# Index planes turned a tile at a time, and constant products ahead of TensorE's waits

## The reference, cut to what matters

```python
sc = einsum('thid,ikd->thik', q, keys)               # 8 heads, 2 halves, 128 keys each
top_s, top_i = top_k(sc, 16)
cand_s = top_s[:, :, 0, :, None] + top_s[:, :, 1, None, :]
best_s, best_pos = top_k(cand_s.reshape(c, 8, -1), 16)
idx = ...                                            # expert i * 128 + j
gate = softmax(best_s)
act = gelu(einsum('td,thkd->thk', xc, u[idx]))
out = einsum('thk,thkd->td', gate * act, v[idx])
```

## Time and profile before

| | |
|---|---|
| three runs | 2798.41, 2799.45, 2804.3 us |
| profiled execution's own time | 2799.7 us |
| its span | 2798.0 us |
| busy: PE, DVE, ACT, POOL | 2708.4, 1826.1, 927.0, 340.7 us |
| mean granted clock of PE | 0.989 |
| PE busy, 500 to 1160 us | 630.0 of 660 |
| PE busy, 1320 to 1430 us (groups of layer 0) | 104.7 of 110 |
| PE busy, 1430 to 1850 us (main loop of layer 0) | 416.5 of 420, DMA share 0.93 |
| TensorE's wait for ScalarE (L2637) before 1315.89 us, early blocks | 2.00 us |
| POOL's last gather issue before the one-hots | 1313.41 us |

### The profile page before, as it was taken

One profiled execution on the slowest core, in us unless ns is written; L12 is line 12 of the kernel. 1 busy time (PEld: TensorE's weight loads), 2 busy tenths in 40 slices (PEclk: granted clock), 3 DMA queues, 4 the chain that ended last, 5 costly groups with the idle time before them and its releaser, 6 DMA issues.

```text
span 2798.0 us, 46131 instructions
## 1 busy us (share of the span) xinstructions
PE 2708.4 (97%) x17120; PEld 2473.6 (88%) x17120; DVE 1826.1 (65%) x3984; ACT 927.0 (33%) x1975; POOL 340.7 (12%) x409
## 2 busy tenths in 40 slices
PE   8999999999999899998999999999999989999998
PEld 4888888778888788898999999977889989999998
DVE  6888888746665687679854454447867887445442
ACT  4222222324674566412521110126752144111001
POOL 0000000000000000001831121100000156111210
PEclk9999999999999999999999999999999999999999
DMA  7333233222323233369469999942344865999995
GB/s 300 112 122 127 106 122 142 71 95 96 136 73 109 91 117 139 125 232 381 177 247 383 378 395 420 402 145 106 113 153 174 347 231 196 358 379 376 419 421 195
DMA packets 86356, 609.20 MB, mean 218 GB/s; under 512 B 9584, under 2 KB 9968, under 8 KB 13744
## 3 DMA queue, kind: packets, MB, share of 16 engines
q1 hardware_dynamic: 60480, 420.23, 39.9%
q0 software_dynamic: 25712, 186.79, 16.9%
HBM read 605.93 MB, written 1.05 MB: 217 GB/s over the span
## 4 chain that ended last, share of the span: by engine, by line
PE 83%; DVE 9%; issue 3%; ACT 2%; DVEq 2%; DMA 1%; ACTq 0%; POOL 0%; POOLq 0%
PE bank L2538 21%; PE bank L504 10%; PE bank L506 10%; PE bank L505 10%; PE bank L2528 7%; PE bank L2477 4%; PE bank L2500 4%; PE bank L2513 3%; PE bank L1690 3%; DVE arena L2582 1%; PE bank L1007 1%; PE bank L996 1%; PE bank L1380 1%; PE bank L1398 1%; DVE res L2587 1%
## 5 line engine op out<-in xcount | busy, mean ns | idle before, releaser
L2538 PE MATMUL bank<-arena,wring 128*128 128x176 f32 x4096 | 626.4, 313 | 4.0 <-DVE arena L2860 4.0
L2538 PEld LDWEIGHTS bank<-arena,wring 128*128 128x128 f32 x4096 | 614.4, 190 | 6.8 <-issue 6.3
L488 DVE TENSOR_TENSOR peer_r<-wring,peer_r 128x512 fp32r<-128x512 f32 x440 | 296.2, 697 | 213.2 <-ACT peer_r L483 210.0
L504 PE MATMUL bank<-h_r,peer_r 128*128 128x512 f32 (+1 forms) x1088 | 395.9, 364 | 4.9 <-DVE h_r L518 3.3
L2595 POOL DMA_INDIRECT arena<-in_experts,arena x160 | 174.7, 1092 | 1718.8 <-DVE arena L2813 1001.7
L506 PE MATMUL bank<-h_r,peer_r 128*128 128x512 f32 (+1 forms) x1088 | 383.6, 353 | 0.0
L483 ACT ACTIVATE peer_r<-wring 128x512 fp32r<-128x512 f32 x440 | 266.6, 628 | 231.1 <-PE bank L506 225.9
L505 PE MATMUL bank<-h_r,peer_r 128*128 128x512 f32 (+1 forms) x960 | 333.0, 347 | 0.0
L2582 DVE SCALAR_TENSOR_TENSOR arena<-arena,res 128x1024 f32<-128x1024 f32 x128 | 156.8, 1225 | 267.9 <-DMA arena<-in_experts,arena 266.6
L2477 PE MATMUL bank<-res,wring 128*128 128x176 f32 x1920 | 288.1, 313 | 4.0 <-ACT arena L2637 4.0
L2477 PEld LDWEIGHTS bank<-res,wring 128*128 128x128 f32 x1920 | 286.6, 190 | 5.3 <-issue 4.8
(11 more groups left out here) (423 smaller groups left out, 4031.4 us busy)
## 6 DMA issues: line engine op xcount, KB each, us to landing
wring<-in_w_peer SPq DMA_DIRECT2D x256, 1024.0 KB, 8.1
wring<-in_w_proj SPq DMA_DIRECT2D x34, 1024.0 KB, 4.8
wring<-in_w_hy SPq DMA_DIRECT2D x32, 1024.0 KB, 5.0
arena<-in_w_ada POOLq DMA_DIRECT2D x16, 1024.0 KB, 5.0
wring<-in_w_out SPq DMA_DIRECT2D x16, 1024.0 KB, 4.8
wring<-in_w_ada SPq DMA_DIRECT2D x8, 1024.0 KB, 9.8
wring<-in_w_hyout SPq DMA_DIRECT2D x8, 1024.0 KB, 4.8
wring<-in_w_q SPq DMA_DIRECT2D x8, 1024.0 KB, 4.8
```

Source lines behind the costliest of these rows:

```text
L488: v.tensor_tensor(SPLIT[:, buf, 1, :], raw_quarter(name, i, j, q), SPLIT[:, buf, 0, :].bitcast(F32), ALU.subtract).then_inc(split_lo, 1)
L504: pe.matmul(out_ap, w_hi, x_hi, start=start, stop=False, **kw)
L2538: mm = pe.matmul(expert_sum(k), w[:, k * P:(k + 1) * P], gates, start=False, stop=True, skip_group_check=True)
```

## The change

New places of constant products: 5 ahead of the last `back` of the convolution, 3 between heads and `at_out`, 4 ahead of norm0, and in each layer 2 between `values_tensor` and split chunk 4, 3 ahead of the norm behind the mixer, 3 between the fold and the norm behind the experts.

In the expert layer the planes of tile 0 are turned and copied on their own, right behind the planes products in the middle of the early blocks. `pair_ready` counts tiles. VectorE makes the one-hots of groups 0 and 1 behind part 14 of `route(1)`, so ahead of the last L2790. GpSimd makes its own when tile 0 is there. ScalarE makes them behind the last early block, then copies tile 1. TensorE turns tile 1 ahead of group 2. VectorE and GpSimd wait for tile 1 from group 12 on. The tables TV, TIU, TIF of the routing move 4096 words further, out of the way of the one-hots.

```diff
-        c6 = Carve(BLOCKS * T)
+        c6 = Carve(BLOCKS * T + 2 * UNITS * UNIT)
...
-            hyena_tiles(pe, head, tail, back, first=first)
+            hyena_tiles(pe, head, tail, back, first=first, ahead_of_last=lambda: keep_clock(pe, 5, 5))
...
         def norm0_tensor(pe):
+            keep_clock(pe, bank_of("at_out", 0, KT - 1)[0], 4)
             tokens_tensor(pe, 0, "at_out")
...
                 mm.then_inc(fold_done, 1)
+            keep_clock(pe, 4, 3)
             tokens_tensor(pe, 2 * l + 2, f"post{l}")
...
             values_tensor(pe, l)
+            keep_clock(pe, bank_of(f"proj{l}", 0, 4)[0], 2)
             proj_split(pe, l, 4)
...
+            def pair_turn(tt):
+                pe.wait_ge(ijg_ready, 2 * l + tt + 1)
+                for q in range(3):
+                    mm = pe.transpose(bank[2 + tt][:, q * P:(q + 1) * P], IJG[:, q, tt * P:(tt + 1) * P], ident)
+                mm.then_inc(ijt_done, 1)
...
                 if n == PLANES_AFTER:
                     planes()
-
-            pe.wait_ge(ijg_ready, 2 * (l + 1))
-            for tt in range(2):
-                for q in range(3):
-                    mm = pe.transpose(bank[2 + tt][:, q * P:(q + 1) * P], IJG[:, q, tt * P:(tt + 1) * P], ident)
-                mm.then_inc(ijt_done, 1)
+                    pair_turn(0)
...
             for n in range(GROUPS):
                 b, x = n % 4, GROUPS * l + n
+                if n == 2:
+                    pair_turn(1)
                 pe.wait_ge(hot, HOT0 + x + 1)
...
+            def pair_in(tt):
+                act.wait_ge(ijt_done, 2 * l + tt + 1)
+                act.activation(PAIR[:, :, tt * P:(tt + 1) * P], view(bank[2 + tt][:, 0:3 * P], 3),
+                               ACT.Copy).then_inc(pair_ready, 1)
...
+                    pair_in(0)
...
-            for tt in range(2):
-                act.wait_ge(ijt_done, 2 * l + tt + 1)
-                a = act.activation(PAIR[:, :, tt * P:(tt + 1) * P], view(bank[2 + tt][:, 0:3 * P], 3), ACT.Copy)
-            a.then_inc(pair_ready, 1)
-            act.drain()
...
+            act.drain()
             hots_scalar(0)
             hots_scalar(1)
+            pair_in(1)
+            act.drain()
...
-            pool.wait_ge(pair_ready, l + 1)
+            pool.wait_ge(pair_ready, 2 * l + 1)
             for n in range(GROUPS):
+                if n == FIRST_TILE:
+                    pool.wait_ge(pair_ready, 2 * l + 2)
...
+            def hots(n):
+                v.wait_ge(g_done, GDONE0 + GROUPS * l + n + 1)
+                if n == FIRST_TILE:
+                    v.wait_ge(pair_ready, 2 * l + 2)
...
+                if n == LAST_PART:
+                    v.wait_ge(pair_ready, 2 * l + 1)
+                    hots(0)
+                    hots(1)
...
-            v.wait_ge(pair_ready, l + 1)
...
-            hots(0)
-            hots(1)
...
             heads_tensor(pe, OG_PARTS)
+            keep_clock(pe, 4, 3)
             at_out_tensor(pe, OG_PARTS)
...
                 mixer_tensor(pe, l)
+                keep_clock(pe, 7, 3)
                 tokens_tensor(pe, 2 * l + 1, f"out{l}")
```

More of the change, by code:

```diff
@@ L333, in program @@
         TIF = c6.take(2 * ROWS, TOPK)
-        assert c6.at <= BLOCKS * T + 16 * P
+        assert c6.at <= ARENA - 4 * GATHERS - P
         c6 = Carve(WK_AT)
@@ L2419, in program @@
         GROUPS = TD // 4
+        FIRST_TILE = (P - NG) // 4
         MID_STEPS = MID * KT
@@ L2423, in program @@
         kept_pairs = lambda n: G[:, MAIN + MID + 2 * n:MAIN + MID + 2 * n + 2, :].rearrange("p a t -> p (a t)")
-        ROUTE_STEPS = 10
+        ROUTE_STEPS, LAST_PART = 10, 14
         TABLE_STEPS, MAIN_STEPS = 6, 32
@@ L2637, in early, with hots_scalar @@
                 act.activation(kept_pairs(n), bank[b][:, 0:2 * TD], ACT.Gelu).then_inc(bank_free[b], 1)
+            def pair_in(tt):
+                act.wait_ge(ijt_done, 2 * l + tt + 1)
+                act.activation(PAIR[:, :, tt * P:(tt + 1) * P], view(bank[2 + tt][:, 0:3 * P], 3),
+                               ACT.Copy).then_inc(pair_ready, 1)
+            def hots_scalar(n):
+                act.wait_ge(g_done, GDONE0 + GROUPS * l + n + 1)
+                t = 4 * (n % 2) + 1
+                act.activation(NEAR[:, n % 2, :], iota, ACT.Abs, scale=-1.0, bias=pair[:, 2, n // 2, t, :])
+                act.drain()
+                act.activation(OHB[:, t, :], NEAR[:, n % 2, :], ACT.Relu, scale=-1.0, bias=ones[:, 0:1]).then_inc(hot_c, 1)
             for n in range(EARLY // 2):
@@ L2802, in peer_vector @@
                 pass
-            step = -2
+            def hots(n):
+                v.wait_ge(g_done, GDONE0 + GROUPS * l + n + 1)
+                if n == FIRST_TILE:
+                    v.wait_ge(pair_ready, 2 * l + 2)
+                par = n % 2
+                if par:
+                    t = 4 * par
+                    v.tensor_scalar(OHB[:, t, :], iota, pair[:, 2, n // 2, t, :], None, ALU.is_equal)
+                for s in range(4):
+                    t = 4 * par + s
+                    a = v.tensor_scalar(OHA[:, t, :], iota, pair[:, 1, n // 2, t, :],
+                                        pair[:, 0, n // 2, t, :], ALU.is_equal, ALU.mult)
+                a.then_inc(hot, 1)
             for n, _ in enumerate(route(1)):
@@ L2823, in peer_vector @@
                     gather_step(v, l, n - 3)
-            assert n >= 2 + ROUTE_STEPS, n
-            v.wait_ge(pair_ready, l + 1)
+                if n == LAST_PART:
+                    v.wait_ge(pair_ready, 2 * l + 1)
+                    hots(0)
+                    hots(1)
+            assert n == LAST_PART >= 3 + ROUTE_STEPS, n
             v.drain()
```

## The result

The changed kernel takes 2785.04 us (median of five, 2784.83 to 2790.93), the kernel before 2804.3 beside it (2798.41 to 2807.78): ratio 0.9943 [0.9926, 0.9961]. 2785.9 was forecast, in [2778, 2795.5]. The profiled execution took 2790.93 with a span of 2789.3, the slowest of the five, so what it lost on the way is in the rows too.

The account below looks back on a forecast made before the run. TensorE, with 83% of the chain, was taken as the bound, with gains at its pauses and half-clock stretches. Planes 8.0, norms 1.7 and 2.1, chunk 4 2.0 sum to 13.8: 2799.7 becomes 2785.9 us, range 2778 to 2795.5.

Parts of the forecast that it names:

- Index planes, 4.0 a layer: Start of the expert groups: tile 0's planes turned early let group 2 start sooner; 8.0 us for both layers.
- The two last terms: Expert groups: group 2 starts 4.7 us earlier, then 0.7 a layer taken off for VectorE's first gather step.
- Price of a constant product, 0.43: Each added 128x512 f32 product: 0.43 us of TensorE at full clock, 12.0 for 28, free if hidden by a wait.
- The slower rival: Constant products run on TensorE's path: all 28 uncovered cost 12.0 us, giving 2803.7; chance 0.05.
- cover "even at half clock": Argument against products on the path: each group is shorter than its pause even at half clock, as 4.3 < 5.18.
- Norms, 1.7 and 2.1: First norm and norms after the experts: products keep the clock up; half of 3.3 and of 4.1 us taken.
- Chunk 4, 1.0 a layer: Ahead of split chunk 4: pause shrinks to 1.2 us, clock drop gone, mixer returns part; 2.0 together, bounds 0 and 3.4.
- Convolution 0: Convolution end: 0 gained, as TensorE would wait longer for VectorE; that wait could drop the clock, costing up to 1.7.
- heads 0 to 1.7: End of the heads: pause of 2.95 us without a drop in this execution; 0 gained, at best 1.7.
- norm behind the mixer 0: Norm after the mixer: half-clock transposes are off the chain, so 0; bounds -0.5 to +1.
- The expert loop moves along: Expert loop: its transfers start on TensorE's progress, so it would move along and not give the planes' gain back.
- the rival priced by it (2.4 us): GpSimd one-hots hold up VectorE's two instructions, planes 1.2 us later a layer, 2.4 in all: 2788.3; chance 0.06.

Follow-up runs that it names:

- fill_norms: Changed kernel with 8 constant products instead of 4 at norm0, 6 instead of 3 behind mixers and experts: 2795.25 us, 0.997 of the kernel before.

## Why the prediction was right, step by step

**Index planes, 4.0 a layer.** Right in size and in mechanism. Group 0 starts 4.28 us earlier relative to the early blocks (4.4 forecast), group 2 has a pause of 1.7 (1.6 forecast), both end on ScalarE as forecast, and start and groups together win 4.00 and 4.15. The prediction named a wait on VectorE ahead of group 0 as a sign of being wrong. The row shows that label, and the order of the ends above shows that it is not the cause. The two last terms were off in opposite ways. Group 2 starts 8.18 us behind the early blocks (7.8 forecast), so 4.16 and 4.29 earlier than before, not 4.7. Behind it only 0.15 a layer goes back, not the 0.7 put down to VectorE's gather step. Taking away group 2's wait on ScalarE gives 1.2 a layer.

**Price of a constant product, 0.43.** Wrong by a factor of two, the prediction's one false price. The earlier trace rows shows eight records, taken there for eight products; they are four. The price is 0.86 on the chain at full clock and 0.79 in what the groups grew by. So 28 products are 22 to 24 us of TensorE, not 12.0. It did no harm because at the true price, too, each group is shorter than its pause: 5 in the convolution take 4.45 of the 5.18 us, 4 in norm0 3.60 of 4.46, 3 in norm2 2.84 of 3.56. With 0.43 I would have filled the norms twice over, and `fill_norms` shows what that costs. The slower rival rested on the same price. Its point of decision (19 of 28 outside pauses) should be 10 (8.0 / 0.86), and its cover "even at half clock" is false: 5 products would take 8.6 us of the 5.18.

**Norms, 1.7 and 2.1.** Too small, for the same reason. I gave half because 2.7 us of pause would be left in norm0. What is left is 1.03 and 0.79, and the clock held in all twelve kernels. The full 3.3 and 2.9 that I had worked out for norm0 and for layer 0's norm2 stand against 3.14 and 2.69. In the last norm 1.08 is won by TensorE, and 0.73 of it goes back, since ScalarE's L1533 and VectorE's L1539 end last there. Forecast 3.8, measured 6.2.

**Chunk 4, 1.0 a layer.** The two products take 1.72 of the 2.04 us (0.34 is left, where I had 1.2), the drop is gone in every layer, and the stretch to the scores goes from 41.45 to 39.94: 1.5. Then the mixer gives it back, and not by small waits as I wrote: the clock drops some 60 us later, as at 1016.21 in layer 0. The timeline of after there:

```profile
1012.19 0.43 PE L1850 MATMUL bank<-arena 128*64 128x128 f32 x2
...
1015.16 0.73 PE L1884 MATMUL bank<-cum,sel 16*128 16x256 f32 x4 [1.19 <-ACT arena L2059]
```

and the same place before:

```profile
1017.79 0.73 PE L1882 MATMUL bank<-cum,sel 16*128 16x256 f32 x4 [1.19 <-ACT arena L2056]
```

There is a pause of 1.19 us here, with narrow products (64 columns, 16 rows) around it. The kernel before has the same instructions and the same pause, and no drop behind it, so the pause alone doesn't make one. Over the twelve kernels with the products the mixers take 209.67 on average, over the four layers without 210.20: 0.5 a layer. In 13 of the 24 layers the clock drops at this place and the stage is 209.79 or more. In two (`fill_norms`) it is 209.66 and 209.69 without a drop, in the others at most 208.99. What makes the second drop come or stay away isn't shown.

**Convolution 0, heads 0 to 1.7, norm behind the mixer 0.** The convolution's 0 was right, and so was its warning: the longer wait is 2.43 (2.5 forecast) and drops the clock in 4 of 9. I should have given it a mean of -0.7 instead of taking 0. The heads' "partly chance" was right as well: the profiled execution before was the lucky one of four. The norms behind the mixers win nothing, and with 3 products the drop comes a little later and costs 0.8 in 6 of 18. With 6 (`fill_norms`) both together took 57.40 instead of 58.3, the one place where more of them helped; alone that wasn't tried.

**The expert loop moves along.** Not quite. The kept blocks took 424.56 and 424.79 in the two profiled kernels with late planes and 424.80 to 430.50 in the twelve with early ones, 427.4 on average. TensorE's pauses in the kept blocks of after, then of before:

```profile
1634.53 136.55 PE L2545 MATMUL bank<-arena,wring 128*128 128x176 f32 x912 [2.06 <-DVE arena L2873]
1772.57 65.11 PE L2545 MATMUL bank<-arena,wring 128*128 128x176 f32 x432 [1.49 <-DMA wring<-in_w_peer]
...
2568.74 202.40 PE L2545 MATMUL bank<-arena,wring 128*128 128x176 f32 x1344 [2.33 <-DVE arena L2873]
```

```profile
1639.26 201.19 PE L2538 MATMUL bank<-arena,wring 128*128 128x176 f32 x1344 [1.62 <-DVE arena L2860]
...
2578.77 200.72 PE L2538 MATMUL bank<-arena,wring 128*128 128x176 f32 x1344 [2.18 <-DVE arena L2860]
```

The same wait on the gathered rows, a little longer, and once one on a weight's transfer. So about 1.3 a layer may be given back. Two kernels on one side are too few to call it shown.

**The sum.** By the averages: groups 8.2, norms 6.2, chunk 4 1.1, heads 1.3 (the mean over the four without), convolution -0.7, norms behind the mixers -0.5, kept blocks -2.7: 12.9. Forecast 13.8; measured 19.3 and 13.6 by medians. The total was met because the half taken off the norms stood in for losses that I had at 0. That the terms cancel so closely is luck.

**GpSimd and VectorE.** GpSimd's five one-hots took 6.83 us instead of five times 0.6. Their line in that stretch (1313.00 to 1320.50) has minimum, median and maximum in ns:

```profile
L2722 POOL TENSOR_SCALAR arena<-const_t,arena x5: 594/691/2602, 1313.2 to 1319.4; 128x128 f32<-128x128 f32 x5
```

Three take 0.59 to 0.69 us. The two that meet VectorE's L2796 and L2798 take 2.60 and 2.38, and each ends 0.46 to 0.47 us behind the end of VectorE's instruction. VectorE's two took 2.29 and 2.30, as before. The Trainium skill's page "SBUF — State Buffer" (section "SBUF: two separate sides") has the two exclude each other for the whole instruction, whichever starts first. The trace agrees for GpSimd, which finished only behind VectorE; VectorE was not held up, so the rival priced by it (2.4 us) was rightly small.

## What to carry to other kernels

Price a filler by its records: count them against the calls in the source, for a product of f32 may be two instructions. Size the filler a little under the pause, where it left 0.3 to 1.0 us here, and put none ahead of a wait that will only grow, since the longer wait can drop the clock itself. When a row names who ended a wait, check that the waiter needed that very instruction: the label can be that of a later step of the same counter. One profile of a stage that sits at the edge of a clock drop is one throw of a coin: look at several executions before an edit there is booked as 0.

## What the runs showed of the hardware

- A pause of 2.95 us behind the heads left the clock up in one kernel and dropped it in three with the same instructions around it; 2.4 us behind the convolution dropped it in 4 of 9.
- A drop removed at one place came at another within the same stage, in 13 of 24 layers. In the changed kernel it stands behind a pause of 1.19 us that the kernel before passes at full clock.
- A product of 128x512 in f32 is recorded as two instructions, and holds TensorE for 0.86 us.
- A GpSimd one-hot of 0.6 us took 2.60 and 2.38 us where it met VectorE's two instructions of 128x2048, and ended 0.46 to 0.47 us behind them; VectorE's took no longer.
